# Masks, second projections and the scaling of linear attention at other places of a hybrid decoder's first layer

## The chip, the cores and the metric

The kernel runs on one core of a Trainium2 chip. The number that counts is the device time of one execution in microseconds (us), as the median of several runs. A core has five engines that work at the same time and wait for each other by semaphores: TensorE (PE: matrix products), VectorE (DVE), ScalarE (ACT), GpSimd (POOL) and SyncE (SP, which here only issues transfers). In the profile PEld is TensorE's loading of weights, which runs beside the products.

## The reference

Two layers over x, 1024 tokens by 1024 channels, float32. The odd layer (a recurrent block) is not touched by the change. The even layer is:

```
h    = rmsnorm(x, pre_norm)
proj = h @ even_w_in       # aq ak av ag | iq ik iw | bq bk bv bg blr
# (A) sparse softmax attention, 8 heads of 64
score = sum_h iw[t,h] * relu(iq[t,h] . ik[s] / 8)       # token indexer, causal
idx   = top_k(score, 256)
p     = softmax(aq . ak[idx] / 8 + rel_bias[bucket(t - idx)])
a_out = (p @ av[idx]) * silu(ag)
# (B) gated linear attention, 4 heads, in chunks of 64 tokens
g_out = head_rmsnorm(gla_chunked(bq, bk, bv, log_sigmoid(gate) / 16)) * silu(bg)
x     = x + rmsnorm(concat(a_out, g_out) @ even_w_out, post_norm)
```

Attention is computed densely: a key that is not among a query's 256 best gets a large negative number from a mask. Nothing of the arithmetic is altered by the change.

## The kernel before, in words

Everything is written out by hand: each engine has one program, in the order in which its instructions stand, and the semaphores that join them. Nothing is scheduled by a tool. Products in full precision are made of three (`three`, L1718 ff.): high part by high part, and the two mixed ones; the matmuls of projections are at L1721 to L1723. ScalarE makes the high part of each block of weights (`high(c)`, L837 and L820), GpSimd the low part (`low(c)`, L641 and L632), SyncE loads the raw block (`load_raw`), two blocks ahead.

A query block is 128 tokens; there are eight (0 to 7). Blocks 2 to 7 need a mask. The stages that matter:

1. Value tiles. TensorE projects v for both head groups in 24 tiles; ScalarE copies each out of PSUM (L937). At the same time the 256th best score of each query is searched bit by bit. For blocks 2 to 5 VectorE counts (L1340). For blocks 6 and 7 ScalarE does (`sum_signs`, L954), and GpSimd settles each bit (`settle_signs`, L665 to L669): 2 x 32 rounds. The tables `SIGNS_VALUE`, `SIGNS_KEYS` and `SIGNS_GATES` say after which tile or half product how many such rounds stand.
2. The gate half products i = 0 to 15 ("g"), 24 matmuls each, and between them linear attention by tile t: `gla_turn` (L1868, L1873), `gla_update` (L1883), `gla_output` (L1901, L1906). `gla_turn(t)` waits until VectorE has masked the tile before (`gla_mask`, L1380); `gla_update` waits for `gla_state` (L1394). VectorE also makes the attention masks here: `make_mask(qb)` is five passes over the block's scores (L1449 to L1453), and before it, for blocks 6 and 7, `settle_ties` (L1435 to L1444) when all 32 bits are there.
3. Attention: 32 steps, a = 0 to 31, pair of heads p = a // 8, query block qb = a % 8. In step a TensorE computes the scores of step a (`head_logits`, L1813 to L1815), then turns and weighs the probabilities of step a - 1 (`turn` L1954, `weigh` L1970) in groups of up to four key blocks. Between these stand "parts" of the projections of q and k: a half product (p, f), f = 0 to 3, is four parts of six matmuls; f = 2 and 3 hold keys and queries of tokens 512 to 1023, which the pair first needs in its block 4. The table `FILLERS` says how many parts a step takes. All half products but (0, 1) use one PSUM bank, so the next begins when ScalarE (`split_pair`, L1076) and VectorE (`low_pair_result`, L1476) have read the last.
4. The chain inside a step: VectorE masks head 0 (`masked`, L1488), GpSimd puts the relative bias of head 1 over the same mask (`near_bias`, L761), VectorE masks head 1, and TensorE may start the next step's scores only when both are read. GpSimd's program in a step is: `near_bias(a, 1)`, `near_first(a + 1)`, then whatever else stands in the step.
5. The result of linear attention lies in memory (`gla_d`, written at L507). SyncE loads it back in two pieces of 1 MB when all projections are done (`g_back`, L568), GpSimd scales it by the norm in steps 26 to 29 (`scale_gla`, L749), and TensorE turns it in steps 28 to 31 (`turn_gla`, L1983).

SyncE's program is one queue too: a wait in it holds all transfers behind.

## Time and profile before

| | us |
|---|---|
| median of 3 runs (lowest, highest) | 1051.07 (1048.62, 1053.96) |
| the profiled execution | 1050.3 |
| its span (first to last instruction) | 1048.5 |
| TensorE busy | 986.3 (94%) |
| VectorE busy | 628.5 (60%) |
| ScalarE busy | 526.1 (50%) |
| GpSimd busy | 331.6 (32%) |

TensorE is busy nearly all the time, so what matters is where it is not, and where its granted clock is the lower of its two levels (0.5 in the records: 1.2 instead of 2.4 GHz). The rows below give both by stretches. Stretches are in microseconds from the start of the span; the boundaries of attention steps are the starts of their first score matmul.

### The profile page before, as it was taken

To read this page: it belongs to the slowest core of one execution; us is meant where nothing else is said; L and a number is where in the kernel's file an instruction comes from. 1 tells how busy PE (TensorE), PEld (TensorE's weight loads), DVE (VectorE), ACT (ScalarE), POOL (GpSimd) and SP (SyncE) were. 2 spreads that over 40 slices of the span, in tenths; PEclk is the share of its full clock that TensorE was granted. 3 is DMA by queue.
4 is the path that set the end of the run, shared out by engine and by line. 5 is a ranking of instruction groups with operands and counts; after the bars stand their busy time and mean duration, and the time that the engine had idled before them with its cause. 6 is when DMAs were issued, how large, how long until landed. Compare 5 with 4: busy or idle time off the path is not lost.

```text
span 1048.5 us, 15126 instructions
## 1 busy us (share of the span) xinstructions
PE 986.3 (94%) x5706; PEld 801.8 (76%) x5706; DVE 628.5 (60%) x1080; ACT 526.1 (50%) x906; POOL 331.6 (32%) x428
## 2 busy tenths in 40 slices
PE   4998999999997897899999788999999999999997
PEld 3886789998876676677777576888888888888885
DVE  5313889979969334444545461666539494889252
ACT  6423675777665453444555574343437272766221
POOL 1310225346647232413231564210322222215200
PEclk9998999999999899899999898999999999999998
DMA  8252102101232223201010435222321121103152
GB/s 256 61 70 52 42 5 78 41 2 44 67 91 80 66 78 101 62 12 41 17 56 32 153 120 161 87 94 80 96 62 45 41 61 41 42 22 103 55 201 81
DMA packets 71743, 75.86 MB, mean 72 GB/s; under 512 B 5064, under 2 KB 58360, under 8 KB 71672
## 3 DMA queue, kind: packets, MB, share of 16 engines
q1 hardware_dynamic: 70400, 73.30, 22.4%
q10 hardware_dynamic: 1272, 1.62, 1.3%
q8 instruction: 44, 0.72, 0.3%
q14 instruction: 27, 0.22, 0.1%
HBM read 58.13 MB, written 16.25 MB: 71 GB/s over the span
## 4 chain that ended last, share of the span: by engine, by line
PE 58%; DVE 5%; ACT 2%; issue 2%; POOL 1%; DVEq 0%; POOLq 0%; ACTq 0%
PE ps L1721 16%; PE ps L1723 15%; PE ps L1722 15%; PE ps L1970 3%; PE ps L1954 3%; PE ps L1813 1%; PE ps L1906 1%; PE ps L1815 1%; PE ps L1814 1%; DVE prob L1488 1%; PE ps L2031 1%; DVE tmp L1583 0%; ACT pT L1093 0%; DVE xt L1588 0%; DVE rank L1452 0%
## 5 line engine op out<-in xcount | busy, mean ns | idle before, releaser
L1721 PE MATMUL ps<-hH,wH 128*128 128x512 f32 x384 | 157.8, 411 | 7.3 <-DVE qkL L1476 7.3
L1723 PE MATMUL ps<-hH,wL 128*128 128x512 f32 x384 | 151.3, 394 | 0.0
L1722 PE MATMUL ps<-hL,wH 128*128 128x512 f32 x384 | 151.2, 394 | 0.0
L641 POOL TENSOR_TENSOR wL<-raw,wH 128x1024 fp32r<-128x1024 f32 x32 | 79.4, 2486 | 72.4 <-ACT wH L837 71.9
L1721 PE MATMUL ps<-h1H,w_slot_H 128*128 128x512 f32 x256 | 99.8, 390 | 0.0
L1723 PE MATMUL ps<-h1H,w_slot_L 128*128 128x512 f32 x256 | 99.6, 389 | 0.0
L1722 PE MATMUL ps<-h1L,w_slot_H 128*128 128x512 f32 x256 | 99.6, 389 | 0.0
L1340 DVE TENSOR_SCALAR_CACHE_REDUCE junk<-score,cand 128x768 bf16<-128x768 f32 (+3 forms) x128 | 96.6, 809 | 1.1
L1721 PEld LDWEIGHTS ps<-hH,wH 128*128 128x128 f32 x384 | 73.0, 190 | 25.2 <-issue 11.4
L1723 PEld LDWEIGHTS ps<-hH,wL 128*128 128x128 f32 x384 | 72.9, 190 | 16.1
L1722 PEld LDWEIGHTS ps<-hL,wH 128*128 128x128 f32 x384 | 73.2, 190 | 13.0
L638 POOL TENSOR_TENSOR w_slot_L<-raw,w_slot_H 128x1024 fp32r<-128x1024 f32 x16 | 41.3, 2584 | 125.0 <-ACT w_slot_H L833 125.0
L1721 PE MATMUL ps<-wH,hH 128*128 128x256 f32 x256 | 75.4, 295 | 0.0
L1722 PE MATMUL ps<-wL,hH 128*128 128x256 f32 x256 | 72.8, 284 | 0.0
L1723 PE MATMUL ps<-wH,hL 128*128 128x256 f32 x256 | 72.7, 284 | 0.0
L1093 ACT ACTIVATE pT<-ps 128x512 f32<-128x512 f32 (+3 forms) x96 | 42.1, 488 | 58.6 <-PE ps L1954 58.5
L954 ACT ACTIVATE signs<-score,cand 128x1024 bf16<-128x1024 f32 x64 | 70.1, 1096 | 1.8 <-POOL cand L663 1.0
L1082 ACT ACTIVATE prob<-prob,small 128x128 f32<-128x128 f32 (+7 forms) x64 | 49.7, 777 | 34.1 <-DVE small L1494 34.1
L1488 DVE CUSTOM_DVE_ANT_0 prob<-ps,score 128x384 f32<-128x384 f32 (+5 forms) x48 | 42.7, 890 | 33.3 <-POOL score L761 21.7
L761 POOL TENSOR_TENSOR score<-nearm,near 128x256 f32<-128x256 bf16 x48 | 31.8, 676 | 79.7 <-DVE small L1488 79.2
L1723 PEld LDWEIGHTS ps<-h1H,w_slot_L 128*128 128x128 f32 x256 | 48.0, 188 | 10.1
L1721 PEld LDWEIGHTS ps<-h1H,w_slot_H 128*128 128x128 f32 x256 | 48.1, 188 | 10.0 <-issue 0.2
(268 smaller groups left out, 2330.6 us busy)
## 6 DMA issues: line engine op xcount, KB each, us to landing
raw<-in_even_w_in SPq DMA_DIRECT2D x32, 512.0 KB, 3.9
xt<-in_x SPq DMA_DIRECT2D x16, 512.0 KB, 5.5
raw<-in_odd_w_in SPq DMA_DIRECT2D x16, 512.0 KB, 3.9
gate_d<-gst SPq DMA_DIRECT2D x16, 256.0 KB, 2.2
raw_row<-in_even_w_out SPq DMA_DIRECT2D x8, 512.0 KB, 3.4
x_d<-xt SPq DMA_DIRECT2D x8, 512.0 KB, 2.6
raw_row<-in_odd_w_out SPq DMA_DIRECT2D x8, 512.0 KB, 3.3
xt<-x_d SPq DMA_DIRECT2D x8, 512.0 KB, 4.7
```

The costliest lines, as they stand in the source:

```text
L638: pool.tensor_tensor(w_slot_L[s][:, :, :], raw[:, c % 2, :, :], w_slot_H[s][:, :, :].bitcast(F32), ALU.subtract).then_inc(w_lo, 1)
L641: pool.tensor_tensor(wL[:, s, :, :], raw[:, c % 2, :, :], wH[:, s, :, :].bitcast(F32), ALU.subtract).then_inc(w_lo, 1)
L761: pool.tensor_tensor(dst, nearm[:, qb, NEAR - w:NEAR], near[:, p % 2 * 2 + e, NEAR - w:NEAR], ALU.add).then_inc(near_ready, 1)
L954: act.activation(signs[:, 0:(qb + 1) * P], score_of(qb), ACT.Sign, bias=cand[:, col].bitcast(F32), scale=-1.0, accum_out=cnt[:, col]).then ...
L1082: act.activation(prob[:, i, 0:w], prob[:, i, 0:w], ACT.Exp, bias=nmx[:, c:c + 1], accum_out=lsum[:, c:c + 1]).then_inc(exp_done[e], 1)
L1093: act.activation(pT[:, e, 0:m * P], ps[:, TURN_BANK[e], 0:m * P], ACT.Copy).then_inc(turn_out, 1)
L1340: return steps(dve.tensor_scalar(junk1[:, j % 2, 0:(qb + 1) * P], score_of(qb), threshold, None, op, ALU.add, accum_out=dst[:, j:j + 1]))
L1488: dve.tensor_tensor_reduce(out=prob[:, i, 0:w].rearrange("p (b w) -> p b w", b=banks), in0=ps[:, b:b + banks, 0:wb], in1=mask_of(qb).rearr ...
L1721: pe.matmul(dst, lH, rH, start=k == 0, stop=False)
L1722: pe.matmul(dst, lH, rL, start=False, stop=False)
L1723: return pe.matmul(dst, lL, rH, start=False, stop=k == nk - 1)
L1954: last = pe.transpose(ps[:, TURN_BANK[e], i * P:(i + 1) * P], prob[:, buffer_of(n, e), (first + i) * P:(first + i + 1) * P], ident[:, :])
```

## The change

Five things are moved; no instruction of the computation goes away, and one ScalarE instruction and four pairs of transfers are added.

- All masks before attention. VectorE's ties of block 7 and `make_mask(7)` move from step 0 to the end of the gate stage, `gla_mask` and `gla_state` of a tile now stand between single masks, and the rounds of the bit search are spread so that they end sooner: 36 instead of 24 in the value tiles, 12 as before beside the keys, 16 instead of 28 beside the gates (the last after half product 9, formerly 13).
- Each pair's f = 2 and f = 3 go into its own first two steps with four parts each, and the steps of blocks 6 and 7 take none. So the last pair's steps 24 and 25, formerly without parts, have four each.
- Linear attention is scaled in steps 4 to 7: SyncE loads two tiles (512 KB) into the new buffer `g_two`, GpSimd scales them, SyncE stores them, and loads the next two when the store has landed, four times. The wait in SyncE's program for the first product of the pairs is now one for linear attention's last product. `g_back` is loaded scaled, and TensorE waits for the load instead of GpSimd.
- The last projection's weights are split by GpSimd in steps 26 to 33, formerly 25 to 32; ScalarE's part keeps its place between the last exponent of a step and the first copy of the next.
- After the root for the norm ScalarE runs one small Exp, which loads that table at this place.

```
-    SIGNS_VALUE = [1] * (3 * NT)
+    SIGNS_VALUE = [2, 1] * (3 * NT // 2)
-    SIGNS_GATES = [2] * 14 + [0, 0]
+    SIGNS_GATES = [2] * 6 + [1] * 4 + [0] * 6
...
-    for a, count in enumerate([4, 4, 2, 2, 2, 2, 4, 4] + [2] * 16):
+    for a, count in enumerate([4, 4, 2, 2, 2, 2, 0, 0] * 3 + [4, 4]):
...
         sp.wait_ge(bias_out, 16)
-        sp.wait_ge(proj_full, nth_product("pair", 0, 0) + 1)
+        sp.wait_ge(att_full, 2 * NT)
...
         sp.wait_ge(gla_norm, 1)
         sp.dma_start(odd_par, odd_channels).then_inc(par_in, 16)
+        for t in range(2):
+            sp.wait_ge(gla_out[t], 16 * NT // 2)
+        for u in range(NT // 2):
+            two = gla_d[2 * u * P:(2 * u + 2) * P, :].rearrange("(t p) n -> p t n", p=P)
+            if u:
+                sp.wait_ge(scaled_out, 16 * u)
+            sp.dma_start(g_two[:, :, :], two).then_inc(two_in, 16)
+            sp.wait_ge(gla_scaled, 2 * u + 2)
+            sp.dma_start(two, g_two[:, :, :]).then_inc(scaled_out, 16)
...
         def scale_gla(t):
             pool.wait_ge(gla_norm, 1)
-            pool.wait_ge(g_back_in[t // 4], 16)
-            gn = g_back[t // 4][:, t % 4, :].rearrange("p (h n) -> p h n", h=B_HEADS)
+            pool.wait_ge(two_in, 16 * (t // 2 + 1))
+            gn = g_two[:, t % 2, :].rearrange("p (h n) -> p h n", h=B_HEADS)
...
-            if 26 <= a < 30:
+            if 4 <= a < 8:
                 for t in range(2):
-                    scale_gla(2 * (a - 26) + t)
+                    scale_gla(2 * (a - 4) + t)
...
-            if 25 <= a < 33:
-                low(C_WOE + a - 25)
+            if 26 <= a < 34:
+                low(C_WOE + a - 26)
...
+        act.activation(small[:, 26:27], epst, ACT.Exp)
...
         gla_mask(3)
         make_mask(2)
+        gla_state(3)
         make_mask(3)
-        gla_state(3)
+        gla_mask(4)
         make_mask(4)
-        gla_mask(4)
+        gla_state(4)
+        gla_mask(5)
         make_mask(5)
-        gla_state(4)
-        for t in (5, 6):
-            gla_mask(t)
-            gla_state(t)
+        gla_state(5)
+        settle_ties(1)
+        make_mask(6)
+        gla_mask(6)
+        gla_state(6)
+        settle_ties(0)
         gla_mask(7)
-        settle_ties(1)
+        make_mask(7)
         gla_state(7)
-        make_mask(6)
...
-            if a == 0:
-                settle_ties(0)
-                make_mask(7)
...
-            pe.wait_ge(gla_scaled, 4 * hf + 4)
+            pe.wait_ge(g_back_in[hf], 16)
```

VectorE in the gate stage, before, from the end of the mask of block 3 on: `state` is `gla_state(3)`, the five rows with 128x640 are the mask of block 4, `att` is `gla_mask(4)`.

```order
L1453 TENSOR_SCALAR score<-rank 128x512
L1394 SCALAR_TENSOR_TENSOR state<-state,small,ps 128x128 x4
L1449 TENSOR_SCALAR eqt<-score,cand 128x640
L1450 SCALAR_TENSOR_TENSOR rank<-small,eqt 128x640
L1451 SCALAR_TENSOR_TENSOR rank<-rank,need,eqt 128x640
L1452 SCALAR_TENSOR_TENSOR rank<-score,cand,rank 128x640
L1453 TENSOR_SCALAR score<-rank 128x640
L1380 COPY_PREDICATED att<-tri,ps 128x2x2x128
```

VectorE at the same place in the changed kernel, from `gla_state(3)` to `gla_mask(4)` and on (its line numbers are ten higher):

```order
L1404 SCALAR_TENSOR_TENSOR state<-state,small,ps 128x128 x4
L1459 TENSOR_SCALAR eqt<-score,cand 128x512
L1460 SCALAR_TENSOR_TENSOR rank<-small,eqt 128x512
L1461 SCALAR_TENSOR_TENSOR rank<-rank,need,eqt 128x512
L1462 SCALAR_TENSOR_TENSOR rank<-score,cand,rank 128x512
L1463 TENSOR_SCALAR score<-rank 128x512
L1390 COPY_PREDICATED att<-tri,ps 128x2x2x128
L1459 TENSOR_SCALAR eqt<-score,cand 128x640
```

Before, the masks of blocks 2, 3 and 4 stood between `gla_mask(3)` and `gla_mask(4)`; now those of blocks 2 and 3 do, and `gla_state(3)` stands in front of the second.

TensorE in step 6, before, from the turning of block 5's first four key blocks to the weighing of its last two; after these rows eighteen matmuls of projections follow, the rest of four parts:

```order
L1954 MATMUL ps<-ident,prob 128x128 x8
L1721 MATMUL ps<-hH,wH 128x512
L1722 MATMUL ps<-hL,wH 128x512
L1723 MATMUL ps<-hH,wL 128x512
L1721 MATMUL ps<-hH,wH 128x512
L1722 MATMUL ps<-hL,wH 128x512
L1723 MATMUL ps<-hH,wL 128x512
L1962 MATMUL ps<-ident,rl 128x128
L1970 MATMUL ps<-pT,v 64x128 x8
```

TensorE in step 6 of the changed kernel, from the same turning on, into the scores of step 7:

```order
L1965 MATMUL ps<-ident,prob 128x128 x8
L1973 MATMUL ps<-ident,rl 128x128
L1981 MATMUL ps<-pT,v 64x128 x8
L1965 MATMUL ps<-ident,prob 128x128 x4
L1981 MATMUL ps<-pT,v 64x128 x4
L1824 MATMUL ps<-qkH_117 128x512 x2
```

No projection stands between turning and weighing any more; the parts are in steps 8 and 9.

GpSimd in steps 5 and 6 of the changed kernel, with the semaphores that each row waits for; `near` rows are the biases (the first of a step for head 1, the second for head 0 of the next step), and the rows with `g_two` were not there before:

```order
L770 TENSOR_TENSOR score<-nearm,near 128x256 [waits s_masked0,near_in1]
L776 CAST nearm<-score 128x256 [waits mask_ready]
L770 TENSOR_TENSOR score<-nearm,near 128x256 [waits near_in0,near_base]
L758 TENSOR_TENSOR g_two<-g_two,small 128x512 [waits two_in,gla_norm] x2
L770 TENSOR_TENSOR score<-nearm,near 128x256 [waits s_masked0,near_in1]
```

The scaling has moved in front of the bias of head 1 of the next step, and waits for a transfer.

## Rows read from the trace of the kernel before

**Rows 1.** The page: each engine's busy time, share of span, instructions.

```profile
PE 986.3 (94%) x5706; PEld 801.8 (76%) x5706; DVE 628.5 (60%) x1080; ACT 526.1 (50%) x906; POOL 331.6 (32%) x428
```

**Rows 2.** Timeline of TensorE: start, duration, instruction, [idle before, releaser].

```profile
342.67 0.59 PE L1873 MATMUL ps<-bqk,kdec 64*128 64x128 f32 x2 [7.97 <-DVE att L1380]
...
408.07 0.39 PE L1813 MATMUL ps<-qkH 64*128 64x256 f32 x2 [1.50 <-DVE qkL L1476]
...
421.87 0.77 PE L1721 MATMUL ps<-hH,wH 128*128 128x512 f32 x1 [6.59 <-DVE qkL L1476]
...
489.42 0.47 PE L1721 MATMUL ps<-hH,wH 128*128 128x512 f32 x1 [0.24 <-DVE qkL L1476]
...
585.01 0.55 PE L1970 MATMUL ps<-pT,v 128*64 128x128 f32 x6 [0.74 <-ACT pT L1093]
```

**Rows 3.** Windows: stretch, length, busy time of each engine, granted clock, DMA.

```profile
334.20:347.50 13.30, 5.33 (x53) 3.99 (x51) 12.99 (x13) 2.30 (x4) 5.08 (x3) 0.74 0.23 60
414.30:429.80 15.50, 8.91 (x38) 6.24 (x37) 9.13 (x18) 3.19 (x8) 4.10 (x4) 0.78 0.04 6
475.60:483.30 7.70, 7.70 (x68) 6.03 (x67) 1.82 (x9) 4.48 (x10) 1.36 (x4) 1.00 0.26 69
483.30:487.80 4.50, 4.50 (x29) 3.03 (x27) 3.34 (x12) 1.39 (x5) 3.45 (x3) 1.00 0.28 60
512.00:527.70 15.70, 15.70 (x130) 11.98 (x128) 9.39 (x21) 9.80 (x19) 4.76 (x5) 1.00 0.08 19
579.80:586.00 6.20, 5.05 (x57) 3.94 (x55) 2.30 (x11) 2.97 (x9) 1.06 (x2) 1.00 0.89 318
586.00:589.10 3.10, 1.76 (x17) 1.03 (x15) 1.97 (x11) 1.05 (x4) 1.30 (x2) 1.00 0.14 48
589.10:619.90 30.80, 25.63 (x199) 19.57 (x199) 18.74 (x58) 19.27 (x40) 26.09 (x23) 0.78 0.39 141
613.20:619.90 6.70, 5.98 (x61) 4.58 (x59) 4.87 (x14) 4.93 (x10) 4.85 (x5) 1.00 0.28 97
```

**Rows 4.** Timeline of VectorE, gate stage and step 0.

```profile
328.76 0.49 DVE L1449 TENSOR_SCALAR eqt<-score,cand 128x512 bf16<-128x512 f32 x1
...
333.42 0.61 DVE L1394 SCALAR_TENSOR_TENSOR state<-state,small,ps 128x128 f32<-128x128 f32 x2
...
341.89 0.72 DVE L1380 COPY_PREDICATED att<-tri,ps 128x512 f32<-128x512 int32 x1
...
410.61 0.10 DVE L1435 TENSOR_SCALAR fix<-cand 128x1 f32<-128x1 f32 x1
```

**Rows 5.** Timeline of TensorE in step 1, a run of projection matmuls.

```profile
426.28 0.40 PE L1721 MATMUL ps<-hH,wH 128*128 128x512 f32 x1
...
429.49 0.39 PE L1723 MATMUL ps<-hH,wL 128*128 128x512 f32 x1
```

**Rows 6.** Timeline, last value tiles: ScalarE, and VectorE's next long idle time.

```profile
210.46 1.15 ACT L954 ACTIVATE signs<-score,cand 128x1024 bf16<-128x1024 f32 x1
...
217.86 0.36 ACT L937 ACTIVATE bv<-ps 128x256 f32<-128x256 f32 x1
...
300.20 0.35 DVE L1394 SCALAR_TENSOR_TENSOR state<-state,small,ps 128x128 f32<-128x128 f32 x1 [8.71 <-PE ps L1906]
```

**Rows 7.** Timeline of GpSimd: biases in steps 6 and 7, a split in step 26.

```profile
456.92 0.67 POOL L761 TENSOR_TENSOR score<-nearm,near 128x256 f32<-128x256 bf16 x1 [5.64 <-DVE small L1488]
...
467.57 0.69 POOL L761 TENSOR_TENSOR score<-nearm,near 128x256 f32<-128x256 bf16 x1 [8.88 <-DVE small L1488]
...
596.39 2.36 POOL L632 TENSOR_TENSOR woL<-raw_row,woH 128x1024 fp32r<-128x1024 f32 x1
```

**Rows 8.** Groups by line, 590 to 620: the scaling on GpSimd.

```profile
L749 POOL TENSOR_TENSOR g_back<-g_back,small 128x512 f32<-128x512 f32 x8 | 8.1, 1036 | 0.0
```

**Rows 9.** DMA issues: transfer, queue, count, KB, median us to landing.

```profile
x_d<-xt SPq DMA_DIRECT2D x8, 512.0 KB, 2.6
xt<-x_d SPq DMA_DIRECT2D x8, 512.0 KB, 4.7
```

More of the change, by code:

```diff
@@ L204, in build @@
     a_gate_0 = at("a_gate_0", [P, T], F32, R1 + 8 * KB)
+    g_two = at("g_two", [P, 2, B_HEADS * B_VAL], F32, R1 + 12 * KB)
     g_back = [at(f"g_back{i}", [P, NT // 2, B_HEADS * B_VAL], F32, R2 + off * KB) for i, off in enumerate((8, 24))]
@@ L366, in build @@
     b_gate_in = [sem(f"b_gate_in{j}") for j in range(KD // 2)]
-    g_back_in = [sem("g_back_in0"), sem("g_back_in1")]
+    g_back_in, two_in, scaled_out = [sem("g_back_in0"), sem("g_back_in1")], sem("two_in"), sem("scaled_out")
     b_turned, b_gated = sem("b_turned"), sem("b_gated")
@@ L564, in _ @@
         sp.wait_ge(proj_full, len(PRODUCTS))
-        for t in range(2):
-            sp.wait_ge(gla_out[t], 16 * NT // 2)
+        sp.wait_ge(scaled_out, 16 * NT // 2)
         for i in range(2):
@@ L1100, in _ @@
                     split_pair(p, f)
+            if 26 <= a < 34:
+                high(C_WOE + a - 26)
             groups = blocks_of[a - 1] if 1 <= a <= NW else []
@@ L1117, in _ @@
                 act.activation(lam_e, lam_e, ACT.Exp, scale=-1.0).then_inc(lam_1, 1)
-            if 25 <= a < 33:
-                high(C_WOE + a - 25)
         act.wait_ge(a_gated, 1)
@@ L1989, in _ @@
         pe.wait_ge(o_out, NT)
+        for part in range(2):
+            pair_part(*filler(0).pop(0))
         for a in range(NW + 2):
```

## The prediction

> **What bounds the kernel now.** I read the page first. TensorE is busy for 986.3 of 1048.5 us [rows 1], so the change can only win what is left, 62 us, and what TensorE loses at its lower clock. Next the timeline of TensorE, looking only at instructions with idle time before them. Two stand out: 7.97 us before a product of linear attention, released by VectorE's `gla_mask` at L1380, and 6.59 us in step 1 of attention, released by VectorE's L1476 [rows 2]. Then VectorE's timeline at both places, to see what it did instead. At the first it made masks: that of block 3 from 328.76, the states at 333.42, that of block 4, and only at 341.89 the tile's mask that TensorE needed [rows 4]. At the second it began the ties of block 7 at 410.61 and came back to the projection at 421. Last the windows, which give both stretches with their clock: 0.74 and 0.78 [rows 3]. After idle times of this size TensorE runs at the lower level for some microseconds, so each costs more than itself. The windows of the last pair of heads show a third place: in 589.10 to 619.90 TensorE is idle for 5.2 of 30.8 us at a mean clock of 0.78, and GpSimd is busy for 26.09, the most of all the engines but TensorE [rows 3]. There a step has no projections to fill it, and GpSimd's two scalings of 1.036 us [rows 8] and a split of 2.36 [rows 7] stand in front of the next step's bias.
>
> **The change part by part.** The sum is made against the profiled execution, 1050.3 us (span 1048.5), which is 0.8 under the median.
>
> a) Masks between the tiles of linear attention. `gla_mask(4)` no longer waits for the mask of block 4. VectorE's order is now: mask of block 2, states, mask of block 3, tile. From 328.76 the states take 1.2 (333.42 to the next mask), the mask of block 3 takes 4.66 (328.76 to 333.42): the tile's mask stands at about 334.7 and is done at 335.4, and TensorE, ready at 334.7, waits 0.8 instead of 7.97: -7.1. The clock: the window 334.20 to 347.50 has 5.33 busy, and the same work elsewhere takes some 3.5: -1.8. Further on, the mask of block 4 (at most the 7 us it took here, 334.64 to 341.89 with VectorE and GpSimd both at work) ends at 342.4 and its states at 343.6, where TensorE needs them only after gate half 10, near 344. From there VectorE has slack: ties and mask of block 6, about 10 us together as those of block 7 (410.61 to 421), end near 361, and the tile's mask behind them is needed near 368. Sum -8.9; between -10.5 (none of the waits, nor a later short fall of the clock) and -5 (the mask of block 3 stretched as block 4's was).
>
> b) Step 1. It took 15.5 us, of which TensorE worked 8.91 [rows 3]. Its work at full clock is the 4.5 of step 9, which has two parts, and two parts more. A part is six matmuls of 0.229 (14 distances in 426.28 to 429.49 [rows 5]), 1.37: 7.2. What is late next is the one PSUM bank: the half product f = 3 can't begin before ScalarE (0.6) and VectorE (0.7) have read f = 2, which ended the step before. In step 10 this wait shows with 0.24 [rows 2], behind longer scores and turnings; step 1's are 0.4 shorter, so 0.6. Step 1: 7.8, thus -7.7; between -8.3 and -6.
>
> c) The same wait is new in steps 9, 17 and 25, where f = 3 now follows f = 2 behind short scores: 3 x 0.6 = +1.8; between 0.7 (0.24 each) and 2.7.
>
> d) Steps 6, 7, 14, 15, 22 and 23 have no parts. Turning, ScalarE's copy and weighing are then in a row with nothing between. Without parts the idle time was 1.15 in step 24 (0.74 of it one wait for the copy [rows 2]) and 0.72 in step 30, which had some turnings to fill it [rows 3]. I take 0.9, between the two: 6 x 0.9 = +5.4; between 3.6 (0.6 each) and 6.9 (1.15 each). The parts themselves cost the same wherever they stand.
>
> e) The last pair. Steps 24 and 25 now hold parts: their idle times go (6.20 - 5.05 and 3.10 - 1.76 [rows 3]), -2.5. In steps 26 to 30 GpSimd loses the scaling. Its step was two biases, two scalings and a split, 1.3 + 2.1 + 2.4 = 5.8, the length of steps 26 and 27 (5.5 and 5.8); it becomes 3.7, and the chain scores, mask, bias, mask then sets about 4.3 (3.1 for step 25 with a block less, plus about half a microsecond per block). With 5.2, 5.7 and 6.4 for the next three, where TensorE's own work decides, and 1.5 for one fall of the clock, 27.4 replaces 30.8: -3.4. Together -5.9; between -9 and -2.
>
> f) The scaling in steps 4 to 7. What hides it is GpSimd's idle time (5.64 and 8.88 us before the biases of steps 6 and 7 [rows 7]); what may not be hidden is that it waits for a transfer in front of the next step's bias. One round is load, scaling, store: 4.7 + 2.1 + 2.6 [rows 8, 9] and 0.3 of issues, 9.7. The first can't start before SyncE has passed the loads that wait for GpSimd's split in step 3. With step 0 at zero the steps start at 25.0 (a = 4), 31.2, 38.2, 43.9 and 50.2, and the scalings end at 31.6, 41.2, 50.6 and 60.1. The bias of head 1 is wanted 2.9 into step 6 and 3.1 into step 7 (454.0 to 456.92, 464.5 to 467.57 [rows 7]), at 41.1 and 47.0. So step 6 is just met, and step 7's bias comes 3.6 late, of which 1.1 is slack until step 8 needs it: 2.5; with loads of 4.0 it is 1.3. Step 8 then is 10.4 us long (7.7 and two parts more), and the last scaling ends before step 9 needs its bias. I take +1.9; between 0 and +6. SyncE's later loads, behind the four stores, are wanted in step 10 and later.
> The Trainium skill ("DMA: Bandwidth & Descriptors", Anatomy of one DMA) puts the fixed part of a transfer at about 2.0 us, most of it the receipt of the write; with 1.2 us for 512 KB at the peak of its Bandwidth section a transfer would be 3.2, a round 8.8, and the sum 1.3 us lower. Of the rows the store (2.6) lies below that and the load (4.7) above, and the sum goes by them.
>
> g) More rounds of the bit search in the value tiles. ScalarE has 1.25 us per round (1.15 and the read of the sum) and in the last eight tiles was full: its copy at 217.86 shows no idle time before it, about 1.5 us after its tile was done [rows 6]. Four rounds more there, 5.0 us, against tiles of 2.88: copies slip until TensorE, two tiles ahead, waits for its bank, once 0.5 and once 2.0; a tenth of that early on, where GpSimd is still splitting weights. +2.8; between 0 (the slips are absorbed) and +6 (they bring the clock down too). Behind it VectorE starts its sums of the gates about 4 us later; it is idle for 8.71 at 300.20 waiting for TensorE, which covers that [rows 6]. The rounds taken out of the gate stage save nothing, as ScalarE is not waited for there.
>
> h) At nothing: the Exp table loaded early (it ended before the first exponent as it was), the biases' load issued 3 us earlier (the first score waits 1.50 for L1476, not for it [rows 2]), ScalarE's splits in steps 26 to 33 (same place), GpSimd's one step later (ready before the last products; should they be late, 2.4 each).
>
> Sum: -8.9 - 7.7 + 1.8 + 5.4 - 5.9 + 1.9 + 2.8 = -10.6, so 1039.7 for the profiled execution. I predict 1040.
>
> **The rivals.** About 0.5%, 5.3 us, is what a measurement of this kernel can tell from no change.
>
> R1, slower than before: the round trip of the scaling is not 9.7 but 14.5 us, because the loads share the queues with weights and gates. Then the scalings end at 31.6, 46.1, 60.6 and 75.1. Step 7 starts 3.9 late, step 8 another 8.6, step 9 another 3.4: 15.9 instead of 1.9, and the time is 1054. It decides from a round of about 14 us. For it: GpSimd's program is in order, and VectorE, TensorE and the next step hang on each bias. Against: no transfer of this size took so long in the median, and the queues are nearly idle in step 6 or 7.
>
> R2, the gain is eaten by the bare steps: without parts six steps are set by the chain from mask to bias to mask, as steps 26 and 27 were with near 1.9 idle each. 6 x 1.9 = 11.4 instead of 5.4, time 1046. For it: the masks are longest there. Against: step 30, almost as long and bare, had 0.72.
>
> R3, a larger gain: neither value tiles nor round trip show (-4.7) and the clock stays up in the last pair (-1.5): 1033.5.
>
> **How the numbers follow.** Chances: the forecast 0.65 (its own range 1036 to 1045), R2 0.15, R3 0.14, R1 0.06. The range 1032 to 1047 leaves out R1 and the ends of R2 and R3, together under 2 in 10. Faster by over 0.5%, under 1045.8: the forecast, R3 and a few hundredths of R2, 0.81; within 0.5%: 0.13; slower: R1, 0.06.
>
> **What would show it.** a) TensorE's wait before the product released by `gla_mask` falls to about a microsecond, and no clock of 0.74 around it. b) Step 1 near 8 us. c) and d) small waits for L1476's successor in steps 9, 17, 25, and 0.9 idle per bare step. e) Steps 26 and 27 near 4.3. f) GpSimd's scaling ending later than the bias was wanted in step 7 alone. g) two waits of TensorE in the last value tiles, for ScalarE's copies. It is wrong if steps 5 to 8 take over 4 us more than given here, if bare steps idle 2 us, or if TensorE still waits for a tile's mask.

## The result, and the profile after

| kernel | median us | runs | ratio to before, 95% interval |
|---|---|---|---|
| before | 1050.37 | 1048.62 to 1053.96 | |
| changed | 1039.93 | 1038.73 to 1043.11 | 0.9901 [0.9879, 0.9923] |

The kernel is 10.4 us faster. The changed kernel also has a sixth move that its description leaves out: TensorE runs two of step 0's four parts ahead of the scores of step 0 (run 1, without this, shows that step 1 doesn't depend on it). The profiled execution of the changed kernel is the slowest of its four (1043.11, span 1041.3), so the traces differ by 7.2 us only. The windows of the changed kernel, cut at the same places of the program as those of before (columns as in [rows 3]):

```profile
91.70:302.09 210.39, 205.79 (x1386) 177.64 (x1385) 173.42 (x348) 151.26 (x247) 94.79 (x212) 0.99 0.15 39
302.09:390.30 88.21, 85.42 (x594) 67.23 (x598) 75.13 (x133) 38.23 (x112) 34.22 (x38) 0.98 0.28 84
390.30:418.00 27.70, 25.61 (x127) 19.51 (x123) 5.20 (x20) 11.06 (x29) 9.21 (x9) 1.00 0.31 95
418.00:567.00 149.00, 139.03 (x1063) 103.42 (x1062) 69.47 (x230) 76.61 (x169) 49.35 (x62) 1.00 0.21 67
567.00:611.60 44.60, 38.71 (x317) 29.16 (x315) 24.44 (x79) 25.50 (x60) 20.55 (x19) 1.00 0.40 136
611.60:631.25 19.65, 12.44 (x114) 9.85 (x113) 9.97 (x19) 11.86 (x19) 8.23 (x5) 0.85 0.26 83
```

The same places before:

```profile
90.70:297.90 207.20, 204.59 (x1386) 176.90 (x1384) 175.00 (x348) 138.08 (x223) 85.73 (x176) 0.99 0.15 39
297.90:394.70 96.80, 87.05 (x594) 68.56 (x598) 60.88 (x117) 52.09 (x136) 43.39 (x74) 0.95 0.25 77
394.70:429.80 35.10, 27.00 (x127) 20.56 (x123) 15.56 (x37) 10.86 (x28) 9.50 (x9) 0.90 0.28 78
429.80:579.80 150.00, 149.30 (x1111) 111.33 (x1110) 72.99 (x231) 77.35 (x172) 41.46 (x54) 1.00 0.12 38
579.80:619.90 40.10, 32.44 (x269) 24.53 (x267) 23.01 (x78) 23.29 (x53) 28.44 (x27) 0.83 0.45 161
619.90:637.60 17.70, 11.19 (x114) 8.58 (x113) 8.20 (x19) 13.02 (x22) 8.26 (x5) 0.98 0.22 69
```

Line by line: from the first value product to the first output of linear attention; to its last output; to step 2; steps 2 to 23; steps 24 to 30; the end of attention. Reading down the lengths: +3.2, -8.6, -7.4, then -1.0 and +4.5, and +1.9. The middle two must be read with the counts of matmuls: 48 fewer stand in steps 2 to 23 and 48 more in steps 24 to 30. That is eight parts of six, 11.0 us by 1.37 each. With them moved back, steps 2 to 23 cost 10.0 more than before, and steps 24 to 30 6.5 less. The rest of the span is +1.0 ahead of the first row and -0.8 behind the last.

TensorE's waits in the changed kernel (timeline, columns as in [rows 2]):

```profile
223.06 0.36 PE L1732 MATMUL ps<-wH,hH 128*128 128x256 f32 x1 [1.43 <-ACT bv L946]
...
339.02 0.72 PE L1884 MATMUL ps<-bqk,kdec 64*128 64x128 f32 x8 [0.21 <-DVE att L1390]
...
341.19 0.45 PE L1912 MATMUL ps<-state,bqk 64*64 64x128 f32 x8 [0.85 <-ACT kn L1035]
...
411.69 0.47 PE L1732 MATMUL ps<-hH,wH 128*128 128x512 f32 x1 [0.59 <-DVE qkL L1486]
...
451.66 1.09 PE L1981 MATMUL ps<-pT,v 128*64 128x128 f32 x16 [0.63 <-ACT pT L1103]
...
455.83 0.39 PE L1824 MATMUL ps<-qkH 64*128 64x256 f32 x2 [0.76 <-DVE small L1498]
...
593.92 0.42 PE L1824 MATMUL ps<-qkH 64*128 64x320 f32 x2 [1.18 <-DVE small L1498]
...
622.10 0.48 PE L1973 MATMUL ps<-ident,rl 128*128 128x128 f32 x1 [2.24 <-DVE rl L1511]
```

The 7.97 and the 6.59 of [rows 2] are gone. At the first place TensorE waits 0.21 for `att`, and then 0.85 for ScalarE's `kn`. At the second 0.59 is left, for the half product in front. New are the 1.43 in the value tiles, two waits of 0.63 (or 0.53) in each bare step (one without parts), 0.76 behind a bias that GpSimd brings late, and a wait of 2.24 in the tail that the prediction did not have.

That last one is read from the timelines of the changed kernel around it. VectorE:

```profile
619.89 2.15 DVE L1511 COPY rl<-small 128x128 f32<-128x128 f32 x1
```

and GpSimd:

```profile
619.62 2.34 POOL L641 TENSOR_TENSOR woL<-raw_row,woH 128x1024 fp32r<-128x1024 f32 x1 [1.99 <-ACT woH L829]
```

The copy takes 0.23 us when GpSimd is idle. Here GpSimd's split of the output weights began 0.27 earlier, and the copy ended at 622.04, 0.08 after the split's end at 621.96. TensorE waited for it, and behind that wait its clock was mostly the lower one (0.56 from 622.1 to 626). The split stands at this instant because part h moved it by one step.

### The profile page after: what moved, and what is told of

Read it like the earlier page. It is cut to its first block, busy times and chain, and to the rows that moved or that the text cites. A ratio compares the mean times of both kernels' runs of the same rounds, so it can differ in the third digit from the quotient of the medians.

```text
span 1041.3 us, 15136 instructions
## 1 busy us (share of the span) xinstructions
PE 982.8 (94%) x5706; PEld 799.6 (77%) x5706; DVE 630.5 (61%) x1080; ACT 525.8 (50%) x907; POOL 331.2 (32%) x428
## 4 chain that ended last, share of the span: by engine, by line
PE 67%; DVE 3%; ACT 3%; issue 2%; DMA 2%; POOL 1%; ACTq 0%; POOLq 0%; DVEq 0%
PE ps L1732 19%; PE ps L1734 19%; PE ps L1733 19%; PE ps L1981 3%; PE ps L1965 2%; PE ps L1917 1%; ACT pT L1103 1%; PE ps L1824 1%; DMA g_two<-gla_d 1%; ACT qkH L1086 1%; DVE qkL L1486 1%; PE ps L1912 1%; DMA gla_d<-g_two 1%; PE ps L2044 1%; PE ps L1825 1%
## 5 line engine op out<-in xcount | busy, mean ns | idle before, releaser
L647 POOL TENSOR_TENSOR w_slot_L<-raw,w_slot_H 128x1024 fp32r<-128x1024 f32 x16 | 41.3, 2582 | 125.0 <-ACT w_slot_H L842 125.0
L1732 PEld LDWEIGHTS ps<-wH,hH 128*128 128x128 f32 x256 | 49.6, 194 | 10.5 <-issue 10.5
L1733 PEld LDWEIGHTS ps<-h1L,w_slot_H 128*128 128x128 f32 x256 | 48.1, 188 | 9.9
```

Of the source, the lines that this page charges most:

```text
L647: pool.tensor_tensor(w_slot_L[s][:, :, :], raw[:, c % 2, :, :], w_slot_H[s][:, :, :].bitcast(F32), ALU.subtract).then_inc(w_lo, 1)
L1732: pe.matmul(dst, lH, rH, start=k == 0, stop=False)
L1733: pe.matmul(dst, lH, rL, start=False, stop=False)
```

## The experiments

Each run is told with its ratio to the kernel before on the same chip. The kernel before was 1049.46, 1049.73, 1048.94 and 1049.22 us in the four groups (1 to 4, 5 to 8, 9 and 10, 11 and 12), and 1050.37 beside the changed kernel. A difference between two kernels of different groups, the changed kernel's too, is the difference of their medians as they stand. Since the kernel before moves by up to 1.4 us from group to group, such a difference is known to about that much.

### 1. The masks alone

The kernel before with VectorE's new order and the new tables of rounds:

```
-    SIGNS_VALUE = [1] * (3 * NT)
+    SIGNS_VALUE = [2, 1] * (3 * NT // 2)
-    SIGNS_GATES = [2] * 14 + [0, 0]
+    SIGNS_GATES = [2] * 6 + [1] * 4 + [0] * 6
...
-        make_mask(4)
-        gla_mask(4)
+        gla_mask(4)
+        make_mask(4)
...
-            if a == 0:
-                settle_ties(0)
-                make_mask(7)
```

> The kernel before with the new order of masks (parts a and b) and the new tables of bit-search rounds (g), and nothing else. Theory: the parts add, and these three carry the whole gain: -8.9 for the tile's mask, -7.7 for step 1, +3 for the value tiles, so 13 to 14 us under before, about 1037, lower than the changed kernel itself; TensorE idles for under 1 us before the product that waits for gla_mask, step 1 has no wait of several us, and the first output of linear attention begins 3 to 4 us later than before. Rival: step 1 only got short because two of its projection parts stand ahead of the attention now; then the wait stays at some microseconds here and the gain is about 7 us, 1043.

Measured: 1035.95 us (1034.89 to 1037.21), ratio 0.9866 [0.984, 0.9891], a gain of 13.5. The masks and the rounds carry more than the whole gain, and step 1 got short without the two parts ahead of it: its wait is 0.59 here too. The rival falls. It also says that the rest of the change, c to f and h together, costs 3 to 4 us (4.0 between the medians, 3.1 when each is taken against its own kernel before).

### 2. The old table of projection parts in the changed kernel

```
-    ... enumerate([4, 4, 2, 2, 2, 2, 0, 0] * 3 + [4, 4]):
+    ... enumerate([4, 4, 2, 2, 2, 2, 4, 4] + [2] * 16):
```

> The changed kernel with the table of projection parts of the kernel before (parts c, d and half of e undone). Theory: the eight waits of 0.63 us for ScalarE's copy in steps 6, 7, 14, 15, 22, 23 and the three of 0.59 us in steps 9, 17 and 25 go (-9.0), steps 24 and 25 are bare again (+2.5), steps 26 to 28 keep their shorter length: 6 to 7 us under the changed kernel, about 1033.5. Rival: the new table is what kept the clock up in the last pair; then steps 24 to 28 fall to the lower clock again and cost 3 to 4 more, and the time is 1037 to 1040, no difference from the changed kernel.

Measured: 1033.54 us (1031.68 to 1034.75), ratio 0.9835 [0.9809, 0.9861]: 6.4 under the changed kernel. Steps 24 and 25 are bare again with 1.15 and 1.35 idle, and the clock did fall behind them. The windows of step 8, of steps 26 to 29 and of step 26 alone:

```profile
462.40:470.10 7.70, 7.70 (x70) 6.03 (x69) 1.82 (x9) 4.48 (x10) 2.81 (x4) 1.00 0.77 239
575.80:594.70 18.90, 17.28 (x142) 12.93 (x142) 14.72 (x46) 14.75 (x31) 13.95 (x12) 0.82 0.52 180
575.80:579.70 3.90, 3.64 (x20) 2.47 (x21) 2.41 (x11) 3.17 (x8) 1.85 (x3) 0.50 0.00 0
```

The rival had the clock right and its price wrong: at 0.82 these four steps took 18.90 us, in the changed kernel at 1.00 19.50 (below). The lower clock fell on steps 26 and 27. Step 26 took 3.90 us at 0.50, with TensorE busy for 3.64, and 3.90 in the changed kernel at 1.00, with 2.36 busy: the chain from mask to bias sets its length, and a slower TensorE fills its own waits. That holds for these two steps only (see run 9). In step 8 the scaling beside filled steps is free: 7.7 us and no wait, as before the change.

### 3. The scaling at its old place in the changed kernel

```
-            if 4 <= a < 8:
+            if 26 <= a < 30:
...
-            pool.wait_ge(two_in, 16 * (t // 2 + 1))
+            pool.wait_ge(g_back_in[t // 4], 16)
```

and SyncE's four round trips are gone.

> The changed kernel with the scaling of linear attention back in steps 26 to 29 on GpSimd, reading the two loaded halves (part f undone, and the other half of e). Theory: steps 7 and 8 lose 1.2 us of waits and length, steps 26 to 28 go back to 5.5, 5.8 and 6.9 us from 3.9, 4.6 and 5.1, so +3.4 to +4.6, in all 2 to 4 us over the changed kernel, about 1043. Rival: with steps 24 and 25 filled GpSimd has a lead when it comes to the scaling, and the bias is not late: then nothing is lost at the end, and the kernel is 1 us under the changed one, 1039.

Measured: 1046.94 us (1045.36 to 1047.99), ratio 0.9964 [0.9949, 0.9979]: 7.0 over the changed kernel, where 2 to 4 was expected. The sign was right and a mechanism was missing. GpSimd in this kernel:

```profile
587.01 1.30 POOL L762 TENSOR_TENSOR score<-nearm,near 128x256 f32<-128x256 bf16 x2 [6.74 <-DVE small L1490]
590.30 2.03 POOL L750 TENSOR_TENSOR g_back<-g_back,small 128x512 f32<-128x512 f32 x2 [1.99 <-DMA g_back<-gla_d]
592.29 2.34 POOL L633 TENSOR_TENSOR woL<-raw_row,woH 128x1024 fp32r<-128x1024 f32 x1
594.59 1.30 POOL L762 TENSOR_TENSOR score<-nearm,near 128x256 f32<-128x256 bf16 x2
```

and SyncE's queue:

```profile
584.72 0.93 SPq L569 DMA_DIRECT2D g_back<-gla_d  x2
```

SyncE issues this load only after the last projection product (`proj_full`), since the buffer lies over weights. The new table puts that product at the end of step 25 instead of 23, so the scaling in step 26 has to wait for its input, and the bias of step 27 comes behind 1.99 of wait, 2.03 of scaling and 2.34 of split, 6.1 us into the step (588.5 to 594.59) where the changed kernel has it after 3.0 (589.3 to 592.28); TensorE waited 4.30. The two parts of the change belong together: with the new table, scaling in the last pair has to wait for its input.

### 4. The rounds of the bit search at their old places in the changed kernel

```
+    SIGNS_VALUE = [1] * (3 * NT)
+    SIGNS_GATES = [2] * 14 + [0, 0]
```

> The changed kernel with the bit-search rounds where they were before (one in each value tile, two in each gate half up to the fourteenth: part g undone). Theory: the wait of 1.43 us before a value tile and about 1.7 us of small delays go (-3); but the counts for blocks 6 and 7 are complete four gate halves later, near 380 us, so their ties and masks (10 us each) run into the first projections and first attention steps: TensorE waits some microseconds for VectorE around 400 us, and the time is 2 to 8 us over the changed kernel. Rival: VectorE had so much slack that the later counts cost nothing; then the time is 3 us under the changed kernel, 1037.

Measured: 1058.7 us (1056.53 to 1060.91), ratio 1.0081 [1.0057, 1.0106]: 18.8 over the changed kernel, more than twice the far end of what was expected. VectorE:

```profile
377.09 0.15 DVE L1445 TENSOR_SCALAR fix<-cand 128x1 f32<-128x1 f32 x1 [18.93 <-POOL cand L675]
```

and TensorE:

```profile
387.39 1.01 PE L1884 MATMUL ps<-bqk,kdec 64*128 64x128 f32 x6 [16.03 <-DVE att L1390]
```

I had looked for the loss behind the gates. It falls inside them: the ties of block 6 stand ahead of a tile's mask in VectorE's program, the count comes at 377, and the tile waits with it. So part g, for 3 us in the value tiles, is what allows a and b.

### 5. Parts spread evenly

Neither table is best. Each pair's second products may end in its own step 1, and no step need be bare:

```
-    ... enumerate([4, 4, 2, 2, 2, 2, 0, 0] * 3 + [4, 4]):
+    ... enumerate([4, 4] + [2] * 24):
```

> The changed kernel with one change: its projection parts are spread as four in steps 0 and 1 and two in each of steps 2 to 25, so that no step is bare and f = 3 never directly follows f = 2 behind short scores. Theory: a part between turning and weighing hides ScalarE's copy; the twelve waits of 0.63 (or 0.53) us and three of 0.59 go, -9, and steps 24 and 25 stay filled and the clock stays up: 9 us under the changed kernel, 1031, and 2.5 under the one with the old table. Rival: with two parts in steps 24 and 25 GpSimd's bias is late at step 26 instead, or the second parts of a pair come too late for its step 4; then the time equals that of the old table, 1033.5.

Measured: 1033.24 us (1032.75 to 1033.58), ratio 0.9827 [0.9801, 0.9853]: 6.7 under the changed kernel, and not to be told from the old table. In the trace the expected waits are gone. TensorE is busy for all of steps 24 and 25 and of steps 6 to 8:

```profile
442.80:466.20 23.40, 23.40 (x198) 18.04 (x197) 10.23 (x32) 11.90 (x27) 9.87 (x13) 1.00 0.29 100
```

and the trace is 9.5 us shorter than that of the changed kernel. The 9 of the theory stands against that trace, which was the slowest of four; against medians it is 6.7. The extra 2.5 over the old table came in part: from step 0 to the end of attention it is 214.3 us here (407.2 to 621.5) and 215.7 there. By step 26 2.3 us are won, and 0.7 given back in steps 26 to 29 (19.6 us here at full clock, 18.9 there), where the chain rules. The medians don't resolve it.

### 6. The output weights' splits one step earlier

```
-            if 26 <= a < 34:
-                low(C_WOE + a - 26)
+            if 25 <= a < 33:
+                low(C_WOE + a - 25)
```

and ScalarE's `high` likewise, back at the end of its step.

> The changed kernel with the splits of the even layer's output weights where they were before, one step earlier (a part of the change that I costed at nothing). Theory: the copy to rl on VectorE, 2.15 us long in the changed kernel because GpSimd's split began 0.27 us before it, takes 0.23 again; TensorE's wait of 2.24 us at the last turning and the lower clock behind it go: 2 to 5 us under the changed kernel, about 1036.5. Rival: the splits now collide with another VectorE instruction of the last steps, or the weights' loads set the place anyway; then no difference, 1040.

Measured: 1045.21 us (1042.4 to 1046.29), ratio 0.9945 [0.9922, 0.9969]: 5.3 slower than the changed kernel where a gain was expected. My theory was right only on the tail (the end of attention), where the copy takes 0.23 and the stretch is 17.7 us long again. It fell in steps 26 to 29. ScalarE at the start of step 26:

```profile
584.32 1.06 ACT L829 ACTIVATE woH<-raw_row 128x1024 fp32r<-128x1024 f32 x1 [3.77 <-PE ps L1734]
585.28 0.58 ACT L1086 ACTIVATE qkH<-ps 128x512 fp32r<-128x512 f32 x1
```

and GpSimd in steps 26 and 27:

```profile
588.50 1.30 POOL L770 TENSOR_TENSOR score<-nearm,near 128x256 f32<-128x256 bf16 x2 [0.70 <-DVE small L1498]
591.82 2.36 POOL L641 TENSOR_TENSOR woL<-raw_row,woH 128x1024 fp32r<-128x1024 f32 x1 [2.02 <-ACT woH L829]
594.13 1.31 POOL L770 TENSOR_TENSOR score<-nearm,near 128x256 f32<-128x256 bf16 x2
```

The same place in the changed kernel:

```profile
587.81 1.30 POOL L770 TENSOR_TENSOR score<-nearm,near 128x256 f32<-128x256 bf16 x2 [6.75 <-DVE small L1498]
589.07 2.38 POOL L641 TENSOR_TENSOR woL<-raw_row,woH 128x1024 fp32r<-128x1024 f32 x1
592.28 1.30 POOL L770 TENSOR_TENSOR score<-nearm,near 128x256 f32<-128x256 bf16 x2 [0.84 <-DVE small L1498]
```

ScalarE issues the split at the end of a step, so GpSimd's half of it comes ready just when the next bias is wanted, and stands in front of it: VectorE waits 2.38 for that bias. Issued at the start of a step, it fits into the gap between two biases. And in step 26 ScalarE's half stands in front of the copy of the last product, so that `qkL`, `rl` and TensorE are late (a wait of 2.42). The windows of steps 26 to 29, here and in the changed kernel:

```profile
584.10:608.10 24.00, 18.68 (x141) 14.13 (x141) 13.70 (x43) 14.21 (x29) 14.55 (x12) 0.79 0.70 238
```

```profile
585.40:604.90 19.50, 14.93 (x141) 11.07 (x140) 14.78 (x44) 14.60 (x30) 14.18 (x12) 1.00 0.82 283
```

From step 26 to the end of attention the two traces differ by 2.4 us (+4.4 in steps 26 to 29, -2.0 behind them), and the programs are the same ahead of that. The rest of the 5.3 between the medians isn't explained by the traces.

### 7 and 8. Both edits, and a milder table of rounds

Run 7 is the edits of 5 and 6 together. Run 8 adds `SIGNS_VALUE = [2, 1] * NT + [1] * NT` and `SIGNS_GATES = [2] * 10 + [0] * 6`.

> The changed kernel with both edits: parts spread evenly, and the output weights' splits one step earlier. Theory: both gains add, -9 and -3: 1028. Rival: steps 26 to 30 have other lengths with the even table, the collision of split and copy is a matter of chance, and the second edit gives nothing or costs 2: 1031 to 1033.

> The same as the run before it, and the table of bit-search rounds with two and one in the first sixteen value tiles, one in the last eight, and two in the first ten gate halves, so that the counts are complete at the same gate half. Theory: ScalarE is not over-full in the last eight value tiles; the wait of 1.43 us at 223 and the smaller ones go, -1.5 to -2.5, so about 1026. Rival: the four rounds put into gate halves 6 to 9 make ScalarE late there for kn and the gates; then no difference or 2 us slower, 1028 to 1030.

Measured: 1034.12 us (1031.76 to 1036.45), ratio 0.9838 [0.9812, 0.9863], and 1033.59 us (1031.82 to 1034.27), ratio 0.9824 [0.9798, 0.9851]. Run 7 is its rival's case, and a little over the 1031 to 1033 given for it: steps 26 and 27 took 5.9 and 5.8 us, as in run 6. Run 8 missed its 1026 and the 1028 to 1030 of its rival, as both were worked out from the 1028 that run 7 didn't reach. The milder table took away the wait of 1.43 as meant, but the difference of 0.5 us can't be told from none.

### 9. Only the seventh split moved, to the end of step 32

On the table of run 5. ScalarE's part:

```
-            if 26 <= a < 34:
+            if 26 <= a < 34 and a != 32:
                 high(C_WOE + a - 26)
...
+            if a == 32:
+                high(C_WOE + a - 26)
```

> The kernel with evenly spread parts (1033.2), and of the output weights' splits only the seventh moved, from the beginning of step 32 of ScalarE's program to its end. Theory: GpSimd's split no longer starts 0.3 us before VectorE's copy to rl; the copy takes 0.23 instead of 2.15 us, TensorE's wait of 2.24 and one stretch of 6.8 us at the lower clock go: 2 to 5 us less, 1029 to 1031. Steps 26 to 28 keep 3.9, 4.6 and 5.2. Rival: the split now stands later in GpSimd's queue, the eighth behind it, and the first output product waits for it, or it stretches VectorE's last multiplications instead: 1033 or more.

Measured: 1031.11 us (1029.1 to 1033.01), ratio 0.9827 [0.9812, 0.9843]. The median is 2.1 under run 5, but the ratio to the kernel before is the same (0.9827), and the spans of the two traces differ by 0.9. In the traces step 31 to the end of attention takes 18.6 us for 19.8. So a gain of about 1 us is likely, and the medians don't show it. Both were right in part. The copy takes 0.23 again and the wait of 2.24 is 0.31, but two splits now stand back to back, and the first output product waits for the later:

```profile
620.73 0.77 PE L1734 MATMUL ps<-woH,msH 128*128 128x512 f32 x1 [5.61 <-POOL woL L641]
```

The changed kernel waited 3.45 for `msL` there.

Up to step 32 the program is that of run 5, so the two traces also show what the clock costs. It fell in step 28 of run 9 and not in run 5:

```profile
583.75:589.60 5.85, 5.85 (x46) 4.91 (x46) 4.07 (x13) 3.87 (x7) 4.88 (x4) 0.71 0.76 246
```

```profile
584.02:589.18 5.16, 4.32 (x45) 3.55 (x45) 4.47 (x14) 3.99 (x8) 4.19 (x4) 1.00 0.73 251
```

Here the lower clock costs 0.7 us. Runs 12 and 11 differ likewise: 5.87 at 0.71 and 4.76 at 1.00. In step 28 TensorE has little idle time to fill.

### 10. The scaling late, with the old table and the splits at their new place

The edits of 2 and 3 together.

> The changed kernel with the old table of projection parts and the scaling back in steps 26 to 29: so the masks (a, b, g) and the output weights' splits at their new place (h). Theory 1: it is the scaling that lengthens steps 26 to 28, and the new place of the splits only brings the slow copy in the tail: 1 to 3 us over the run with the masks alone (1036.0), 1037 to 1039; steps 26 and 27 stay at 5.5 and 5.8. Theory 2, after the run with the splits put back: a split issued at the end of a step stands in front of the next bias and is what lengthens steps 26 to 28, with or without the scaling; then steps 26 to 28 are short here too (3.9, 4.6, 5), and the time is that of the run with the old table, 1033.5 to 1035.

Measured: 1036.11 us (1034.83 to 1036.75), ratio 0.9871 [0.9856, 0.9886], 0.2 over run 1 and 2.6 over run 2 (0.7 and 3.1 when each is taken against its own kernel before). The time lies between the two theories. Steps 26 to 29, beside the 18.90 of run 2:

```profile
575.70:597.90 22.20, 16.44 (x142) 12.48 (x142) 13.50 (x45) 13.87 (x30) 20.32 (x20) 0.92 0.44 153
```

GpSimd is busy for 20.32 of 22.20, in run 2 for 13.95 of 18.90. So the scaling does lengthen these steps, by 3.3, and taking it off is worth 2.6 us in the medians; theory 2 falls. Theory 1 had steps 26 and 27 at 5.5 and 5.8; they took 3.4 and 5.7, so the new place of the splits does shorten step 26. Against run 1 it gains 1.5 us in steps 26 to 29 (22.1 for 23.6) and loses 1.8 in the tail (19.7 for 17.9), which together is the nearly equal time. The lengths of steps 26 to 29 give the account of both moves: 23.6 us with neither (run 1), 22.1 with the splits moved alone (run 10), 24.0 with the scaling moved alone (run 6, on the new table), 18.9 with both (run 2). Neither move alone is worth more than 1.5 us there, and the two together 4.7.

### 11 and 12. The seventh split in the middle of step 32

On the table of run 5, run 12 with the milder table of rounds as well:

```
                 if a < NW:
                     exponent(a, i)
+                if a == 32 and i == 0:
+                    high(C_WOE + a - 26)
```

> As the run before with the seventh split moved, but it stands in the middle of ScalarE's step 32, between the two copies of turned blocks, instead of at its end. Theory: GpSimd has it done before the eighth, so the wait of 5.61 us for woL at the first output product falls back to the 3.45 for msL, and the copy to rl still stays short: 2 us under that run, about 1029. Rival: between the copies it delays the second copy and TensorE with it by 1 us, and the split on GpSimd meets other work of VectorE: no better than that run, 1031.

> The same with the milder table of bit-search rounds (two and one in the first sixteen value tiles, one in the last eight, two in the first ten gate halves). Theory: the wait of 1.43 us at a value tile goes and nothing comes back: 1 to 2 us less than the run before it. Rival: as in the first try of this table the difference cannot be told from none.

Measured: 1028.53 us (1026.46 to 1029.89), ratio 0.9787 [0.9757, 0.9816], and 1027.01 us (1025.52 to 1027.43), ratio 0.9772 [0.9744, 0.98]. GpSimd in run 12:

```profile
607.83 2.35 POOL L641 TENSOR_TENSOR woL<-raw_row,woH 128x1024 fp32r<-128x1024 f32 x1 [3.94 <-ACT woH L829]
```

VectorE:

```profile
606.15 0.23 DVE L1513 COPY rl<-small 128x128 f32<-128x128 f32 x1
```

and TensorE:

```profile
614.26 0.76 PE L1734 MATMUL ps<-woH,msH 128*128 128x512 f32 x1 [3.45 <-DVE msL L1586]
```

The copy is done 1.4 us before the split begins, and the last split ends at 613.04, before `msL` is there. Run 11 is 4.7 us under run 5 between the medians, for one split moved by half a step. In the traces step 31 to the end of attention takes 16.4 us for 19.8, so 3.3 us come from the split; the other 3.1 by which the traces differ lie ahead of it, where the programs are the same. Run 12 is the fastest kernel here, 12.9 us under the changed kernel and 22.2 under the one before it in its group; its 1.5 us over run 11 are at the edge of what the two ranges of runs can tell.

## Why the prediction was right, point by point

The time (1040 against 1039.93) is better than its terms, and that the two are 0.07 apart is luck. Against the profiled execution, for which the sum stood at 1039.7, it is 3.4 us too low (1043.11). The terms, from the windows and waits above:

| term | predicted | traces |
|---|---|---|
| a) masks between tiles | -8.9 | -8.6 |
| b) step 1 | -7.7 | -7.4 |
| c) to step 23, d), f): steps 2 to 23 | +8.5 | +10.0 |
| e) and c) in step 25: steps 24 to 30 | -5.3 | -6.5 |
| g) value tiles | +2.8 | +3.2 |
| h) in the tail | 0 | +1.9 |
| elsewhere | 0 | +0.2 |

- **a) and b)** came by the mechanism given. TensorE's wait for `att` fell to 0.21 (0.8 was expected), the window 334.20 to 347.50 is at full clock, and step 1 took 7.9 for 7.8. Run 1 shows that they and the rounds stand alone, run 4 that they need the rounds. Inside a) two misses cancel: the wait was shorter, and the clock fell once later, near 360:

```profile
355.00:365.00 10.00, 8.27 (x52) 6.49 (x50) 4.55 (x14) 3.93 (x13) 3.57 (x2) 0.83 0.36 107
```

  In the trace of run 2, whose program is the same here, the clock stayed up and the stretch took 86.5 us for the 88.1 here (from output to output, 302.09 to 390.15): a) would then be -10.1, near the end of its own range.
- **c)** came as given, three waits of 0.59 for 0.6 each.
- **d)** was mis-sized: 0.9 per bare step was taken between step 24 (1.15) and step 30 (0.72). The bare steps idle 1.16 and 1.26, each twice for ScalarE's copy, 7.26 in all for 5.4. Step 30 was the wrong end to lean on, since turnings fill it. R2's 1.9 appeared only in step 7 (2.02), where GpSimd's scaling adds to it.
- **e)** was too small by 1.2. Steps 26 to 28 took 3.9, 4.6 and 5.1 us for 4.3, 4.3 and 5.2, and the clock did not fall in this execution, for which I had left 1.5; that was R3's point. What I did not see is that this length rests on h: GpSimd without the scaling, but with the splits at their old place, takes 24.0 us for steps 26 to 29 (run 6), no better than the 24.2 of before. So the step of my argument that took the scaling off and got 3.7 and 4.3 us from that alone is wrong, though the sum came out.
- **f)** The scalings end at 435.5, 445.2, 453.7 and 462.2, which with the steps' zero at 403.9 (two parts stand ahead of step 0) is 31.6, 41.3, 49.8 and 58.3 for 31.6, 41.2, 50.6 and 60.1. The bias of step 6 was just met. That of step 7 was late, and, against what I had written, that of step 8 too, which came at 462.11 behind the fourth scaling. The timeline of GpSimd, and VectorE's wait in step 8:

```profile
433.42 2.04 POOL L758 TENSOR_TENSOR g_two<-g_two,small 128x512 f32<-128x512 f32 x2
...
443.19 2.04 POOL L758 TENSOR_TENSOR g_two<-g_two,small 128x512 f32<-128x512 f32 x2 [3.70 <-DMA g_two<-gla_d]
...
451.65 2.04 POOL L758 TENSOR_TENSOR g_two<-g_two,small 128x512 f32<-128x512 f32 x2 [4.42 <-DMA g_two<-gla_d]
453.65 0.67 POOL L770 TENSOR_TENSOR score<-nearm,near 128x256 f32<-128x256 bf16 x1
...
460.12 2.04 POOL L758 TENSOR_TENSOR g_two<-g_two,small 128x512 f32<-128x512 f32 x2 [5.41 <-DMA g_two<-gla_d]
...
462.67 0.29 DVE L1498 CUSTOM_DVE_ANT_0 prob<-ps,low_mask 128x128 f32<-128x128 f32 x1 [4.59 <-POOL low_mask L770]
```

  VectorE waits 4.59 us for that bias, and 0.52 at the same place of run 3, yet TensorE has four parts to work on and doesn't wait for it. The first round took 9.8 us (433.42 to 443.19), as I had it, and the next two 8.5: the loads took 4.2, 4.8, 3.5 and 3.5, the stores 2.8. Together it cost 1.2 us in steps 6 to 8 (24.5 against 23.3 without it in run 3) for 1.9. The Trainium skill's fixed cost of a transfer ("DMA: Bandwidth & Descriptors", Anatomy of one DMA) is given there for transfers that GpSimd issues, while SyncE issued these. My estimate of 8.8 for a round from it was near two of the three, but its 3.2 for one transfer met neither the loads nor the stores. The "1.3 us lower" doesn't follow either: by the prediction's own steps a round of 8.8 makes the bias of step 7 late by 2.2, less the slack of 1.1, which is 0.8 under the 1.9 (and nothing is left of it if the first load is put at 3.2 as well). R1, with its round of 14.5, is excluded by these rows.
- **g)** as predicted, with one clear wait of 1.43 and one of 0.34; run 4, with the old rounds, takes 207.5 us for this stretch against 210.4.
- **h)** is the step that failed. "At nothing" was said of two things that moved one instruction each on ScalarE and GpSimd, on the ground that both had time. They had; but one split now holds up a copy of VectorE (runs 9 and 11), and the others no longer stand in front of a bias (run 6). In step 26 ScalarE's part did not keep its place either: it now stands behind the copy of the last product. The two effects are +1.9 in the tail and, once the scaling is gone, some -4.5 in steps 26 to 29; the second was hidden in e.

What stays open: why the clock falls behind a wait of 1.0 to 1.2 us at the start of steps 27 and 28 in some executions and not in others (it fell in runs 9 and 12 and not in the changed kernel or in runs 5 and 11, with the same waits), and where the 3.2 us went by which the profiled execution of the changed kernel is over the median. The 1.0 us ahead of its first value product is spread: in runs 5, 9 and 11, whose programs are the same up to there, that product begins at 92.2, 91.6 and 91.0.

## What to carry to other kernels

Undo the parts of a compound change one by one even when it is faster: here the masks with their rounds carried 13.5 us and the rest gave 3 to 4 back. A step without filling work shows its waits (7.3 us in the six bare steps here), so a table should leave as few as it can; two parts in every step are 6.7 us better than the changed table, and can't be told from the old one. Costing a move "at nothing" because its engine has time is not enough: ask which instruction of another engine now runs beside it, and whether it stands before or behind what the next step waits for.

## What was not expected of the hardware

VectorE's copy to `rl` (f32, 128x128, from a broadcast) never overlaps the end of a GpSimd operation that was running when it began. Of the 32 copies in the changed kernel 26 took 0.23 us, the other six 0.60 to 2.15, and each of these ended 0.08 or 0.09 us after GpSimd's instruction did. The kernel before has five such (0.54 to 2.15 us, ended 0.08 or 0.09 after). In all fourteen traces there are 80 among 448 copies; all end 0.07 to 0.10 after an instruction of GpSimd, and all others took 0.23 to 0.29. One of them in the changed kernel, VectorE:

```profile
590.41 1.12 DVE L1511 COPY rl<-small 128x128 f32<-128x128 f32 x1
```

The split beside it ran from 589.07 for 2.38 (above), to 591.45; the copy ended at 591.53. By the Trainium skill ("SBUF — State Buffer", Who interferes with whom) VectorE and GpSimd share a pair of ports as an exclusive lock that a copy can ask for, and the one that comes second is held for the whole instruction; the traces agree to 0.1 us. The operation at L1462 (a comparison and an addition, with two inputs in the same memory) behaves alike. Alone it takes 0.75, 1.02, 1.15 and 1.28 us for 512, 768, 896 and 1024 elements. In the changed kernel's gate stage it took 2.90 for 640, VectorE:

```profile
342.70 2.90 DVE L1462 SCALAR_TENSOR_TENSOR rank<-score,cand,rank 128x640 f32<-128x640 f32 x1
```

while GpSimd ran

```profile
341.94 2.97 POOL L650 TENSOR_TENSOR wL<-raw,wH 128x1024 fp32r<-128x1024 f32 x1
```

It ended at 345.60, 0.69 after GpSimd at 344.91: its own length of about 0.9 less 0.2. For 1024 elements in run 4 (2.18 us, ended 1.08 after GpSimd) and for 896 in the changed kernel (2.04 us, 0.95 after) the same subtraction holds. I had read such lengths in the trace of before as a slowdown by two engines at work; they are waits for the other's end, so a mask's cost beside a split depends on where the split begins.

A lower clock of TensorE was free where another chain set the pace, and not free in the one step compared where TensorE has little idle time. Step 26 took 3.90 us at 0.50 (run 2) and at 1.00 (changed kernel), and step 27 4.59 at 0.64 in run 4 and 4.60 at 1.00. In step 28 it cost 0.7 us (runs 9 and 5) and 1.1 (runs 12 and 11).
